# A two-layer hybrid decoder step, written out layer by layer, with the FFN's products ahead of the norm's scale

## What is computed

```python
def rmsnorm(x, g):
    xf = x.astype(jnp.float32)
    y = xf * lax.rsqrt(jnp.mean(xf * xf, axis=-1, keepdims=True) + EPS)
    return (y * g.astype(jnp.float32)).astype(x.dtype)
def swiglu(h, wg, wu, wd):
    return (jax.nn.silu(h @ wg) * (h @ wu)) @ wd
...
for l in range(DEPTH):
    hdn = rmsnorm(x, ns[0])
    x = x + 0.5 * rmsnorm(swiglu(hdn, gate[0], up[0], down[0]), ns[1])
    hdn = rmsnorm(x, ns[2])
    mix, st_new = token_mixers(hdn, pos, p, st, chunk)
    x = x + rmsnorm(mix, ns[3])
    hdn = rmsnorm(x, ns[4])
    x = x + 0.5 * rmsnorm(swiglu(hdn, gate[1], up[1], down[1]), ns[5])
```

## Time and profile before

| | us |
|---|---|
| median of 3 runs | 1801.04 |
| lowest, highest | 1800.76, 1806.31 |
| profiled execution, first to last instruction (span) | 1796.3 |
| TensorE matmul busy | 1592.9 (89%) |
| TensorE weight load busy (overlaps) | 1492.3 (83%) |
| VectorE busy | 903.6 (50%) |
| ScalarE busy | 556.7 (31%) |
| GpSimd busy | 164.9 (9%) |
| matmuls | 10846 |
| mean granted TensorE clock | 0.871 of full speed |
| share of TensorE in the chain that ended last | 84% |

### The profile page before, as it was taken

One profiled execution on the slowest core, in us unless ns is written; L12 is line 12 of the kernel. 1 busy time (PEld: TensorE's weight loads), 2 busy tenths in 40 slices (PEclk: granted clock), 3 DMA queues, 4 the chain that ended last, 5 costly groups with the idle time before them and its releaser, 6 DMA issues.

```text
span 1796.3 us, 28795 instructions
## 1 busy us (share of the span) xinstructions
PE 1592.9 (89%) x10846; PEld 1492.3 (83%) x10846; DVE 903.6 (50%) x1415; ACT 556.7 (31%) x752; POOL 164.9 (9%) x249
## 2 busy tenths in 40 slices
PE   4999989988787789999889999899788888899995
PEld 3999979977775679999879999799687757799994
DVE  4455455645454555553455544566363544655433
ACT  3333344440011143333353333454200111533331
POOL 6000000100133320000000000001002413000000
PEclk9999999988755589999989999899695556899997
DMA  8455443430011144554334545254101102255440
GB/s 194 149 166 164 159 136 116 148 101 1 3 30 33 12 115 139 164 164 139 117 121 163 164 152 176 71 165 129 48 1 26 26 14 64 95 163 163 142 163 27
DMA packets 184921, 194.17 MB, mean 108 GB/s; under 512 B 7284, under 2 KB 181700, under 8 KB 184688
## 3 DMA queue, kind: packets, MB, share of 16 engines
q1 hardware_dynamic: 176864, 178.27, 30.7%
q0 software_dynamic: 7376, 10.91, 3.5%
q10 hardware_dynamic: 576, 3.59, 0.5%
HBM read 186.55 MB, written 6.19 MB: 107 GB/s over the span
## 4 chain that ended last, share of the span: by engine, by line
PE 84%; DVE 7%; issue 5%; ACT 2%; DMA 1%; DVEq 0%; ACTq 0%; SPq 0%; POOL 0%
PE ps L468 82%; PE ps L471 2%; DVE y L1253 1%; DVE ring_r L1212 1%; DMA ring<-in_ffn_w_up 1%; DMA big<-in_x_sample 1%; DVE y L1670 0%; DVE arena L1483 0%; DVE x L1254 0%; ACT lnr L967 0%; DVE big L1590 0%; DVE big L1709 0%; ACT rrow L968 0%; DVE y L1227 0%; DVE Sbd L1552 0%
## 5 line engine op out<-in xcount | busy, mean ns | idle before, releaser
L1212 DVE TENSOR_TENSOR ring_r<-ring,whigh_r 128x2048 fp32r<-128x2048 f32 (+1 forms) x174 | 389.9, 2242 | 466.4 <-ACT whigh_r L945 466.1
L945 ACT ACTIVATE whigh_r<-ring 128x2048 fp32r<-128x2048 f32 (+1 forms) x174 | 326.2, 1875 | 481.6 <-PE ps L468 471.8
L468 PE MATMUL ps<-hdn,whigh_r 128*128 128x288 f32 x2016 | 328.4, 305 | 24.7 <-ACT hdn L955 15.0
L468 PEld LDWEIGHTS ps<-hdn,whigh_r 128*128 128x128 f32 x2016 | 292.3, 192 | 37.1 <-issue 31.8
L468 PE MATMUL ps<-hdn,ring_r 128*128 128x288 f32 x2016 | 315.9, 300 | 0.0
L468 PE MATMUL ps<-y_r,whigh_r 128*128 128x288 f32 x1888 | 293.4, 299 | 0.0
L468 PEld LDWEIGHTS ps<-hdn,ring_r 128*128 128x128 f32 x2016 | 288.1, 193 | 0.0
L468 PEld LDWEIGHTS ps<-y_r,whigh_r 128*128 128x128 f32 x1888 | 268.8, 191 | 0.0
L468 PE MATMUL ps<-big_r,whigh_r 128*128 128x288 f32 x832 | 130.4, 298 | 7.5 <-DVE arena_r L1212 7.5
L468 PEld LDWEIGHTS ps<-big_r,whigh_r 128*128 128x128 f32 x832 | 117.4, 190 | 8.5 <-issue 8.3
L468 PE MATMUL ps<-big_r,ring_r 128*128 128x288 f32 x704 | 110.9, 299 | 0.0
(11 more groups left out here) (328 smaller groups left out, 1624.4 us busy)
## 6 DMA issues: line engine op xcount, KB each, us to landing
ring<-in_ffn_w_gate SPq DMA_DIRECT2D x44, 1024.0 KB, 5.2
ring<-in_ffn_w_up SPq DMA_DIRECT2D x44, 1024.0 KB, 5.2
ring<-in_ffn_w_down SPq DMA_DIRECT2D x32, 1024.0 KB, 5.1
ring<-in_w_in SPq DMA_DIRECT2D x30, 1024.0 KB, 5.0
ring<-in_ffn_w_down SPq DMA_DIRECT2D x16, 768.0 KB, 4.4
ring<-in_w_out SPq DMA_DIRECT2D x8, 1024.0 KB, 5.4
cst<-in_const ACTq DMA_DIRECT2D x1, 2301.0 KB, 8.3
big<-in_x_prompt ACTq DMA_DIRECT2D x1, 1024.0 KB, 11.4
```

Of the source, the lines that this page charges most:

```text
L468: return pe.matmul(out, lhsT, rhs, start=start, stop=stop, **k)
L945: A(whighR[:, pos % 2, 0:rows * 256], ring[:, s, 0:rows * 256], ACT.Copy)\
L1212: return TT(out, in_, high, ALU.subtract)
```

## The change

The layer loops and the inner loops are written out on every engine, so that slots are counted through both layers (`at(l, pos)`), loads of the next layer follow on without a wait for the layer's end, and per-layer copies of parameters fall away or move into the FFN (`layer_params`, `first_params`). `hold` is a bare wait. The first slot of each stage has a high buffer of its own, SPARE, in tiles 22 to 29 of `big`, and the first two slots of a stage are split before the end of the stage ahead.

Ahead of an FFN, x isn't scaled by the norm: `hdn` and `yR` are the high and low part of x times the gain. The scale, one number per token, is made beside the first pairs, is put on the gate before Silu (`gates`), and is left out of up, since the norm behind the FFN divides by it again; EPS goes into that norm's sum in its place (`eps_ready`). Ahead of the mixers the scaled norm stays. The first two slots of a stage are multiplied together, into four banks, one eighth of `hdn` after the other. The gate and up tiles of a pair alternate between banks 0 to 3 and 4 to 7. Down waits only for the hidden tiles of its part. The scale and the addition to x come in four groups of 1, 2, 2 and 3 tiles. In the opening a small part of the constants and x come first, ring loads don't wait for x, and TensorE starts on products between the transposes. At the end each tile of x is transposed as it is done, and VectorE and ScalarE copy out halves that SyncE stores.

```diff
+X_GROUPS = ((0, 1), (1, 3), (3, 5), (5, 8))
+        SPARE = big[:, 22:30, :].rearrange("p k t -> p (k t)")[:, 0:SLOT]
...
             def load(l, pos, rows, src):
+                gp = at(l, pos)
+                if gp >= RING:
+                    sp.wait_ge(*used(gp - RING))
...
-            sp.wait_ge(sem("x_loaded"), 32)
-            with sp.Fori(0, DEPTH) as l:
+            for l in range(DEPTH):
...
             def hold(s, v):
                 pe.wait_ge(s, v)
-                pe.sem_inc(sem("pe_held"), 1)
...
+            def first_products(l, pos, i, bank, high0, done):
+                w = [weights(l, pos + n) for n in range(2)]
+                slot_ready(l, pos)
+                slot_ready(l, pos + 1)
+                for k in range(KT):
+                    hold(sem("hdn_high"), high0 + k + 1)
+                    for n in range(2):
+                        for t in range(2):
+                            mm(ps[:, bank(n, t), 0:T], w[n][0][:, cut(k, t)], hdnR[:, k, :], k == 0, False)
+                            mm(ps[:, bank(n, t), 0:T], w[n][1][:, cut(k, t)], hdnR[:, k, :], False, False)
+                last_products(l, i, w, bank, done)
...
+            def begin():
+                for k in range(4):
+                    turn(k)
+                hold(sem("weights_high"), 1)
+                for k in range(KT):
+                    hold(sem("hdn_high"), k + 1)
+                    for t in range(2):
+                        mm(ps[:, bank(0, t), 0:T], w[0][0][:, cut(k, t)], hdnR[:, k, :], k == 0, False)
+                    if k < 4:
+                        hold(sem("x_done"), k + 1)
+                        turn(k + 4)
...
+                            if j == 1 and n == 0 and t == 1:
+                                hold(sem("x_summed"), g + 1)
+                                mm(ps[:, 3, 0:T], C("mean"), sq[:, 0, :]).then_inc(sem("norm_sum"), 1)
+                            if j > 1:
+                                hold(sem("up_read" if n else "gate_read"), g * FT + 2 * (j - 2) + t + 1)
...
-                hold(sem("h_done"), l * 44 + f * 22 + 22 + H_CREDIT)
+                        hold(sem("h_done"), g * FT + min(8 * part + 8, FT))
...
             def norm_post(l, post):
-                pe.wait_ge(sem("squares_added"), l * 24 + post * 8 + 8)
-                mm(ps[:, 4, 0:T], ones, ssum[:, :]).then_inc(sem("norm_sum"), 1)
+                hold(sem("squares_added"), l * 21 + post * 7 + 7)
+                mm(ps[:, 4, 0:T], C("mean"), ssum[:, :], True, False)
+                hold(sem("squared"), l * 24 + post * 8 + 8)
+                mm(ps[:, 4, 0:T], C("mean"), sq[:, 1, :], False, True).then_inc(sem("norm_sum"), 1)
...
# ScalarE
+            act.dma_start(cst[:, 0:CONST_HEAD], I["const"][:, 0:CONST_HEAD]).then_inc(sem("const_loaded"), 16)
...
+            act.dma_start(cst[:, CONST_HEAD:], I["const"][:, CONST_HEAD:]).then_inc(sem("consts_loaded"), 16)
...
+            def begin():
+                upper(0, 0)
+                act.wait_ge(sem("gains_placed"), 1)
+                for k in range(KT):
+                    if k == 2:
+                        upper(0, 1)
+                    act.wait_ge(sem("x_done"), x_count(0, k))
+                    scaled_high(0, 0, k)
+                for n in range(4):
+                    x_squares(n)
...
+            def pre_ffn(l, f):
+                for k in range(KT):
+                    act.wait_ge(sem("x_done"), x_count(3 * l + 2 * f, k))
+                    scaled_high(l, 2 * f, k)
+                for n in range(4):
+                    x_squares(n)
...
+                upper(l, base + 2)
+                upper(l, base + 3)
+                pre_scale(l, 2 * f)
                 act.preload_act_table_set("silu_and_others")
+                silus(0)
+                for j in range(1, PAIRS):
+                    upper(l, base + 2 * j + 2)
+                    silus(j)
+                    upper(l, base + 2 * j + 3)
...
# VectorE
+            def pre_ffn(l, f):
+                for k in range(KT):
+                    dve.wait_ge(sem("hdn_high"), l * 24 + 8 * i + k + 1)
+                    STT(yR[:, k, :], x[:, k, :], gn[:, l, 2 * i, k:k + 1], hdn[:, k, :], ALU.mult, ALU.subtract)\
+                        .then_inc(sem("hdn_low"), 1)
+                lower_weights(l, POS_FFN[f] + 2)
+                dve.wait_ge(sem("x_squared"), l * 12 + 4 * i + 4)
+                link(l, TT(xsq[:, 0:4, :], xsq[:, 0:4, :], xsq[:, 4:8, :], ALU.add))
+                link(l, TT(xsq[:, 0:2, :], xsq[:, 0:2, :], xsq[:, 2:4, :], ALU.add))
+                TT(sq[:, 0, :], xsq[:, 0, :], xsq[:, 1, :], ALU.add).then_inc(sem("x_summed"), 1)
+                lower_weights(l, POS_FFN[f] + 3)
+                if g == 0:
+                    first_params()
...
+                def scaled(n):
+                    a, b = X_GROUPS[n]
+                    TT(y[:, a:b, :], y[:, a:b, :], bc(lnr[:, :], 1, b - a), ALU.mult).then_inc(sem("y_scaled"), 1)
...
+                for j in range(1, PAIRS):
+                    gates(j)
+                    lower_weights(l, base + 2 * j + 2)
+                    hidden(j, 0)
+                    hidden(j, 1)
+                    lower_weights(l, base + 2 * j + 3)
```

More of the change, by code:

```diff
@@ L476, in hold, with slot_ready, weights @@
                 pe.wait_ge(s, v)
-                pe.sem_inc(sem("pe_held"), 1)
-            def slot_ready(l, pos, j=0):
-                hold(sem("weights_split"), l * N_POS + pos + 1 + j * 4)
+            def slot_ready(l, pos):
+                hold(sem("weights_split"), at(l, pos) + 1)
             hdnR = hdn[:, :, :].bitcast(F32R)
-            def product(out, pos, t, rows, high, low_, start=True, stop=True, ready=None):
-                wl, wh = ringR[:, pos % RING], whighR[:, pos % 2]
-                cols = [slice(k * 256 + t * P, k * 256 + t * P + P) for k in range(rows)]
+            def weights(l, pos):
+                gp = at(l, pos)
+                return HIGH[gp][1], ringR[:, gp % RING]
@@ L489, in product, with cut @@
+            def cut(k, t):
+                return slice(k * 256 + t * P, k * 256 + t * P + P)
+            def product(out, l, pos, t, rows, high, low_, start=True, stop=True):
+                wh, wl = weights(l, pos)
                 for k in range(rows):
-                    if ready is not None:
-                        hold(sem("hdn_high"), ready[0] + k + 1)
-                    mm(out, wh[:, cols[k]], high[:, k, :], start and k == 0, False)
+                    mm(out, wh[:, cut(k, t)], high[:, k, :], start and k == 0, False)
@@ L493, in product @@
                 for k in range(rows):
-                    mm(out, wl[:, cols[k]], high[:, k, :], False, False)
+                    mm(out, wl[:, cut(k, t)], high[:, k, :], False, False)
                 for k in range(rows):
-                    if ready is not None and k % 4 == 0:
-                        hold(sem("hdn_low"), ready[1] + k // 4 + 1)
-                    g = mm(out, wh[:, cols[k]], low_[:, k, :], False, stop and k == rows - 1)
-                return g
+                    g = mm(out, wh[:, cut(k, t)], low_[:, k, :], False, stop and k == rows - 1)
@@ L501, in _, with last_products @@
+            def last_products(l, i, w, bank, done):
+                for n in range(2):
+                    for t in range(2):
+                        for k in range(KT):
+                            if n == 0 and t == 0:
+                                hold(sem("hdn_low"), low_count(l, i, k + 1 if i != 1 else k // 4 + 1))
+                            g = mm(ps[:, bank(n, t), 0:T], w[n][0][:, cut(k, t)], yR[:, k, :], False, k == KT - 1)
+                        g.then_inc(sem(done[n]), 1)
             pe.sem_inc(sem("sadd_done"), FREE)
@@ L1009, in ffn @@
                         if n >= 2:
-                            upper(l, pos + n, rows, used(l, pos + n - 2))
+                            upper(l, pos + n, rows)
                     if mp:
```

588 lines of the change are left out of this document (305 added, 283 removed).

## The result

| | us |
|---|---|
| before, median of the runs beside it | 1801.43 |
| changed kernel, four runs | 1690.69, 1691.63, 1696.84, 1700.74 |
| its median | 1694.24 |
| ratio, 95% interval | 0.9398 [0.9377, 0.9419] |
| forecast, range | 1715.3, 1697.0 to 1740.0 |

A forecast was written before the change was run, and what follows sets the result against it. TensorE's products set the FFNs' pace, so gains lie only where products stop. Terms 22.7 + 18 + 5 + 10.3 + 15 + 8.7 + 6 = 85.7 us, off 1801.0, gave 1715.3; range 1697 to 1740.

The forecast's parts named there:

- Mixers to second FFN: Norm between mixers and second FFN, twice: second sum and scale leave the path, saving 12.5 and 10.2 us.
- Layer boundary: Between the two layers: written out, the loss falls from 26.2 to 8.2 us, saving 18.0.
- FFN to mixers: Norm between first FFN and mixers, twice: earlier squares and interleaved first products save 2.5 us each, 5; bounds 1 and 10.
- Gate and up to down: Four hand-overs inside the FFNs: no wait for the last hidden tile, 4 x 1.87 + 2 x 1.4 = 10.3 us.
- Opening: Kernel start: earlier ring loads bring the second weight slot at 19 us, saving 15; bounds 5 and 19.
- End: After the last product: x in groups, earlier transposes, last store with the same tail, saving 8.7 us; bounds 5 and 12.
- Waits in the mixers: Bare waits start TensorE 0.09 us sooner at some 39 releases per layer, saving 6 us; bounds 0 and 10.
- The rival with 0.13: Opening: second weight slot not earlier because other loads share the engines; 10 us less gain, 1725.3; chance 0.13.
- VectorE's order: FFN pairs: VectorE's chain makes TensorE wait some 3 us in each of 40 pairs, 1835, slower than before; chance 0.02.
- The clock did fall: Rival at the norms: 4.35 us pause doesn't let the clock fall, 3 x 3.2 us more saved, 1705; chance 0.12.
- the products did start earlier: Rival at the norms: product starts no earlier if x's low parts come late; 4 us less gain each, 1728; chance 0.05.
- the late fetches: Rival on late fetches in straight code, four of them giving the range's end of 1740; chance 0.08.

The follow-up runs named there:

- the second trace: The changed kernel run once more, unchanged, as a base for the experiments: 1697.24 us, ratio 0.9418 [0.9391, 0.9445].

## Why the forecast was wrong

The direction held, and so did the mechanism at the norms and the layer boundary. Two terms failed in kind (the opening, the end), one effect was in no term (the pace), and the sum was too small by 21 us. In the order of the forecast's steps, measured on the profiled executions:

- **Mixers to second FFN** (22.7). Stages shrank by 16.3 and 14.8 us. Less a hand-over with its clock (3.3, as forecast) and the pace (1.2) each, 11.8 and 10.3 are left: 22.1, right. Inside it, the restart was 1.8 us late by the split named above, which the forecast had said was out of the way ("both first slots are split before the end"): they are, but ahead of the last addition.
- **Layer boundary** (18.0). 23.2 less hand-over 1.9 and pace 1.2: 20.1. The low stretch was 3.4 us, not 6.4.
- **FFN to mixers** (5, bounds 1 and 10). From the last product to the end of the 288 projections 80.5 and 82.9 us became 76.0 and 77.2: 10.2, less 0.7 for pace, 9.5. Mis-sized by half: the interleaving alone is 3.1 per layer, where the whole term had 2.5.
- **Gate and up to down** (10.3). The wait is gone everywhere. Undoing it costs 5 to 6 us in the changed kernel; whether its share in the old one was the full 10.3, with the clock, was not tried.
- **Opening** (15, bounds 5 and 19). The stage shrank by 3.7. Less its hand-over (1.9) and the pace (1.2), 0.6 is left for the opening, and 1.7 in the second trace. By the medians of all traces with either opening (257.4 and 249.7) it is 4.6. The step that failed is "I take 19, nearer the first, because that queue stood empty until 14.21". The rival with 0.13, that the second slot is not earlier, is what happened. The queue was not the limit in the changed kernel: GpSimd's small loads held the ring's up, and without them the slot comes at 19.18, the figure the forecast had taken for granted. In the old kernel GpSimd's loads took 51.0% of the engines' time between 24 and 32 us, but holding them back there was not tried.
- **End** (8.7, bounds 5 and 12). 14.5. The step that failed is "the last store with the same tail": SyncE issues the stores and waits for them now, and GpSimd's closing DRAIN of 5 us no longer stands behind them. Moving them back to GpSimd costs 6.1; without that the term is 8.4, right.
- **Waits in the mixers** (6, bounds 0 and 10). 0.09 us per release was right; the count was too small, and places outside the mixers weren't counted. Of the 24.7 us by which the two mixer stages shrank, 13.8 are left after the entry (9.5) and the pace (1.4). The increments alone, taken out of the old kernel, are 9.7 there (with 7 us less at half clock); they cost 10 us in the whole changed kernel and 17 in the old one with TensorE written out.
- **The pace**, in no term: 6.0 us, from where `whigh` lies. The prediction said "Nothing in the change makes a product shorter or fewer".

The spans are 97.4 us apart. From the 85.7 forecast, 14.4 go for the opening and 0.6 for the mixers to the FFN; 5.8 come from the end, 2.1 from the boundary, 4.5 from the entry to the mixers, 7.8 from the rest of the mixers and 6.0 from the pace: 96.9. In this sum the hand-over's 10.3 stands as forecast, not as measured. It is luck that the forecast came as near as it did: the opening's 14 us too much hid more than half of the 26 that the other terms had too little. The medians are 10 us further apart than the spans of the two profiled executions. Runs of the old kernel last 1.6 us beyond their span, so the one of 1796.3 was quick by 3.5 us (the forecast took all 4.7 us for time outside the span), and the changed kernel's was the slowest of four, 6.5 above the median. Why the mixers' clock differs from run to run of one kernel stays open.

Of the other rivals, VectorE's order did not occur: a whole FFN is one piece of the chain. The clock did fall at the norms and the boundary, so that rival was not it either, and the products did start earlier. No run shows the late fetches that have the chance of 0.08 and end the forecast's range at 1740: in the changed kernel's straight code the three whole FFNs are pieces of 213.76, 212.86 and 212.34 us without a pause, and TensorE's loops written out in the kernel before measured 0.9984 [0.9964, 1.0004], so for TensorE's edges this case shows no cost that is clear of the scatter. What VectorE's 6.29 us at "issue" at the layer's edge were, no view shows.

## What to carry to other kernels

Before you credit an earlier issue of a load, look at what else flies then: in a window with a full DMA share and few GB/s look for small loads; moving those (9 to 15 us here) beat moving the load. Take a tail's price with the engine that waits for the last store, since its closing DRAIN comes behind it, and count a second instruction behind each wait of TensorE (0.09 us here) in every stage, not in one. When a change adds or resizes tiles, note where the operands of the main products lie: 32 bytes were worth 6 us, with no line of the products changed.

## What the runs showed of the hardware

- Matmuls of 128x128 by 288 columns start 132.2 ns apart with the stationary high weights' tile at an odd multiple of 64 bytes and 132.9 ns with it 32 bytes off a multiple of 64, in both kernels; a pad of 32 bytes ahead of it alone took them from 132.92 to 132.30 and from 132.18 to 132.95. Products on other weights in the same stream change with them. At a multiple of 128 it is 132.3 to 132.4.
- Beside ten loads of 16 KB (four numbers a piece, L1862) and the small ones behind them, the DMA engines stay at a share of 1.18 and move 83 GB/s; in the same window without them it is 1.05 and 340 GB/s. The weight loads' own packets take 95.0% and 99.3% of the time.
- From the last store's issue to the end of the span: 2.4 us through SyncE, 8.2 through GpSimd, of which GpSimd's closing DRAIN is 5.3 (SyncE's is 0.01).
- An increment behind TensorE's wait adds 0.09 us to a release (medians 0.055 and 0.146).
- Two traces of the same program had 184 and 164 us at half clock in the first mixers; the same 2195 matmuls kept TensorE busy 339.12 and 332.53 us.
